# Half of the mixer's output projection taken into the attention stage, as plain fp32 products with the residual beside them

## The chip, the cores and the metric

One core of one Trainium2 chip runs the whole program. The metric is device time in microseconds (us). Engine names are those of the profile: PE is TensorE, DVE is VectorE, ACT is ScalarE, POOL is GpSimd, SP is the engine that issues most transfers.

## The reference, cut to what matters

The program is a long chain of stages: two mixing blocks over 1024 tokens of 1024 features, then a block with two feed-forward layers and, between them, a mixer with sparse attention. The change concerns the mixer and the residual behind it:

```python
def _mixer(h, w_in, kv_norm_g, w_uk, w_uv, gln_g, gln_b, ws, bs, w_out, topk):
    proj = h @ w_in
    q, c, qi, ki, wi, z = jnp.split(proj, SPLITS, axis=-1)
    ...
    att = _sparse_attention(q, c, qi, ki, wi, w_uk, w_uv, topk)   # 512 features, 8 heads
    gm = _chunked_gmlp(z, gln_g, gln_b, ws, bs)                   # 512 features, "gated"
    return jnp.concatenate([att, gm], axis=-1) @ w_out            # 1024 x 1024

# in second_block, with DEEPNORM_ALPHA = 2 ** 0.25
m = _mixer(x, ...)
x = _layernorm(DEEPNORM_ALPHA * x + m, ln2_g[l], ln2_b[l])
```

So `m = att @ w_out[0:512] + gm @ w_out[512:1024]`. The gated half `gm` depends on nothing that attention computes.

## The kernel before, in words

Activations lie with features on the 128 partitions: `xT` is 128 x 8 x 1024 (eight groups of 128 features, all tokens), and `mT`, the mixer's output, has the same shape. Groups 0 to 3 of `mT` hold the queries and are overwritten, block of 128 tokens by block, with attention's result. Groups 4 to 7 hold the gated half, which is complete when the stage before attention ("in_2") ends.

A dense product is done in three terms. Weights and activations are split into a high part (a copy in the format fp32r, on ACT) and a low part (the remainder, on DVE), and `product` (L280 to L282) issues high x high, high x low and low x high for each group of 128 input features.

**Attention** (`mixer_stage`, block "attention") walks over 8 blocks of 128 queries with 8 heads each, two heads per step: 32 steps and two to drain. Per step s, PE computes the scores of two heads as plain fp32 products over 64 rows (`score`, L3378), turns the probabilities of two heads (`turn`, L3390) and multiplies them with the values (`value`, L3400). DVE adds the mask and finds the minimum (`add`, L3577); ACT does the exponential with its sum (`exponent`, L3486) and copies the turned probabilities out of PSUM (`turned`, L3475). After each block of four steps the inverse sums are turned and spread (L3410, L3417, L3492, L3499) and the block is rescaled (L3589). In the first 16 steps (blocks 0 to 3, "NARROW") each row of scores fits one PSUM bank, four banks rotate, and scores are computed one step ahead of that. From step 16 on a row takes two banks and two rows rotate.

Beside that runs a bitwise search for the top 256 keys of each query of the later blocks. A round is asked on DVE (`rank_ask`, L2966), partly answered on ACT (`sign_round`, L2984), and finished on DVE (L2974, L2976). Which round belongs to which head is fixed beforehand (`ROUNDS_AT`): within steps 0 to 15 there are 20 rounds, and in ten of these steps one lies between ACT's two exponentials.

Each engine works through its own list in the written order and waits at semaphores. Nothing is reordered at run time between the engines' lists.

**The projection** (`combine_stage`, called as "out_2") multiplies `mT` with `w_out`: 16 items, eight output groups for tokens 0 to 511 and then eight for tokens 512 to 1023, each with 8 input groups x 3 terms = 24 products of 512 columns. Per item ACT and DVE cut the weights of the item two further on (L245, L248), DVE adds the result to the residual (`deepnorm_update`, L707: `x = x * ALPHA + product`) and adds up the layer norm's mean (L201, L204). During the second eight items DVE also centres the first 512 tokens (L491), adds their squares (L454, L459), inverts (L497) and scales (L505), as `early_dve` orders. The next stage starts when this has ended.

Of the kernel before, what the change touches and what calls it, by code (L numbers as in the profile page):

```python
# [8 lines left out]
P = 128  # L9
D = 1024  # L10
KD = D // P
# [71 lines left out]
def program(nc, A):  # L83
# [18 lines left out]
    with root:  # L102
# [195 lines left out]

        def load_following(ring, sp, n_tiles, following):
            for m in range(2 if following else 0):  # L300
                ring.load(sp, n_tiles // 2, m, following[m])

# [304 lines left out]

        def combine_stage(name, ring, w_dram, rhs, chunks, groups, update, squares, norm, primed, following, cut=Cut):

            items = [(gi, m) for gi in range(len(groups)) for m in range(KD)]  # L610
            n_items = len(items)
            with ExitStack() as ctx:
                parts = Parts(ctx, name, KD, chunks[-1][0] + chunks[-1][1])
                totals = Totals(ctx, name, chunks, squares, groups)
                norm.totals = totals
                head = cut(rhs, parts, KD, chunks)
                with nc.Block(name) as block:
                    @block.sync
                    def _(sp):
                        for i, (gi, m) in enumerate(items):  # L620
                            if i >= 2 or not primed:
                                ring.load(sp, i // 2, i % 2, w_dram[m])
                            if i == 1:
                                head.on_sp(sp)
                        load_following(ring, sp, n_items, following)

                    @block.scalar
                    def _(act):
                        def finish(i):
                            gi, m = items[i]  # L630
                            if squares:
                                act.wait_ge(evacuated[i % 2].h, evacuated[i % 2].base + i // 2 + 1)
                                totals.square(act, gi, m)
                        steps = in_turn(n_items, lambda i: ring.cut_high(act, i // 2, i % 2), finish, primed, following)
                        head.lead_act(act)
                        next(steps)
                        head.on_act(act, [0])
                        for i, _ in enumerate(steps):
                            if i == 1:
                                head.on_act(act, range(1, len(chunks)))  # L640
                            norm.early_act(act, i, totalled.base)

                    @block.vector
                    def _(dve):
                        def finish(i):
# [11 lines left out]
                        steps = in_turn(n_items, lambda i: ring.cut_low(dve, i // 2, i % 2), finish, primed, following)  # L657
                        head.lead_dve(dve)
# [8 lines left out]
                    def _(pe):  # L667
# [6 lines left out]
                        for i, (gi, m) in enumerate(items):  # L674
# [3 lines left out]
                            for c in groups[gi]:  # L678
# [2227 lines left out]
        def mixer_stage(mT, ring, head, following):  # L2906
# [29 lines left out]
            with ExitStack() as mixer:  # L2936
# [381 lines left out]
                rs = sb(mixer, "at_rs", [P, 2, NH])  # L3318
                rT = sb(mixer, "at_rT", [NH, P])
                N = NQ * NH  # L3320
                PAIRS = N // 2
# [4 lines left out]
                def row_at(n):  # L3326
                    return n % 4 * 512 if n < NARROW else n % 2 * SEQ

                def rows_behind(n):
# [26 lines left out]
                with nc.Block("attention") as block:  # L3356
                    @block.sync
                    def _(sp):
                        sp.dma_start(causal[:, P:2 * P], A["later"]).then_inc(S["a_loaded"], 16)
                        sp.dma_start(xT[0:NH, 4:6, SEQ:T], A["heads_out"].rearrange("h (k j) t -> h k (j t)", k=2))\  # L3360
                            .then_inc(S["a_loaded"], 16)
                        sp.wait_ge(S["a_keys"], NH // 2)
                        load_following(ring, sp, 0, following)

                    @block.tensor
                    def _(pe):
                        def score(p):
                            b, j = p // 4, p % 4
                            if 2 * p < NARROW:
                                if p >= 2:  # L3370
                                    pe.wait_ge(S["a_added"], 2 * (p - 1))
                            else:
                                pe.wait_ge(S["a_added"], 2 * p)
                            for c in range(0, (b + 1) * P, 512):
                                w = min(512, (b + 1) * P - c)
                                for i in range(2):
                                    at, hp = row_at(2 * p + i) + c, slice(64 * i, 64 * i + 64)
                                    last = nc.tensor.matmul(PS[:, at:at + w], mT[hp, j, b * P:b * P + P],  # L3378
# [34 lines left out]
                        def spread_inverse(b):  # L3413
# [4 lines left out]
                            last.then_inc(S["a_transposed"], 1)  # L3418

                        pe.wait_ge(S["a_weights"], 32)  # L3420
                        for k in range(NQ):
# [37 lines left out]
                    def _(act):  # L3459
# [34 lines left out]
                        def inverse_spread(b):  # L3494
                            t = place["spread", b, 0]
                            act.wait_ge(S["a_transposed"], t + 1)
                            if b:
                                act.wait_ge(S["a_rescaled"], b)
                            nc.scalar.activation(spread, bank(4 + t % 2).rearrange("p (k t) -> p k t", k=2), ACT.Copy)\  # L3499
                                .then_inc(S["a_turned"], 1)  # L3500

                        for s in range(STEPS + 1):
                            if 0 <= s - 1 < PAIRS:
                                turned(2 * s - 2)
                                turned(2 * s - 1)
# [10 lines left out]
                            if s - PRIMED_FROM in (0, 1):  # L3516
                                ring.cut_high(act, 0, s - PRIMED_FROM)

                    @block.vector
                    def _(dve):  # L3520
# [48 lines left out]
                        def add(n):  # L3569
# [5 lines left out]
                            if rows_behind(n) >= 0:  # L3575
                                dve.wait_ge(S["a_exp"], rows_behind(n) + 1)
                            nc.vector.tensor_tensor_reduce(  # L3577
                                out=sm[:, at:at + w], in0=PS[:, at:at + w], in1=bias, scale=1.0, scalar=3.0e38,
                                op0=ALU.add, op1=ALU.min, accum_out=mn[:, n % 4:n % 4 + 1]).then_inc(S["a_added"], 1)
# [16 lines left out]
                        for s in range(STEPS + 1):  # L3596
# [21 lines left out]
                            if s - PRIMED_FROM in (0, 1):  # L3618
                                ring.cut_low(dve, 0, s - PRIMED_FROM)
                        link.end()  # L3620


# [106 lines left out]
        with ExitStack() as seam:  # L3729
# [114 lines left out]
```

## Time and profile before

| | |
|---|---|
| three runs | 3782.5, 3794.1 and 3795.0 us, median 3794.1 us |
| profiled execution | span 3783.3 us from the first to the last instruction; the page gives no other time of it |
| attention's steps 0 to 15 | about 2749.8 to 2828.6 us of the span |
| attention's end | about 2964 us |
| the projection, first product to last sum | 2965.6 to 3059 us |
| TensorE's mean granted clock | 0.953 of full |

The start of a stretch is read from the timeline (the first instruction of a line), its work from the windows (busy time per engine and the granted clock in that stretch), and an engine's reason for standing still from the list of waits. Matmuls are pipelined: a row's own duration includes the time for the result to drain, so the rate of a run of matmuls is read from the distance between starts.

### The profile page before, as it was taken

The page shows a single profiled execution, that of the slowest core. Times are in us where ns is not written, and L with a number is a line of the kernel's source. Part 1 is how long each engine was busy: PE and PEld are TensorE (multiplying, and loading weights), DVE is VectorE, ACT ScalarE, POOL GpSimd, SP SyncE. Part 2 cuts the span into 40 slices and gives each one's busy share as a digit, 9 for nine tenths or more (in the row PEclk, how much of TensorE's full clock was granted, in tenths as well). Part 3 has the DMA queues.
Part 4 walks back from the last instruction along what each step waited for, and adds up shares of the span by engine and source line. Part 5 has one row for each costly group of instructions (what it writes and reads, how often), then busy time and mean ns, then how long its engine had stood idle before and what let it go on. Part 6 is the DMA issues. An engine that isn't in the chain of part 4 may idle for free. (4 is left out here: it accounts for less than half of the span.)

```text
span 3783.3 us, 67165 instructions
## 1 busy us (share of the span) xinstructions
PE 3357.8 (89%) x28642; PEld 2684.9 (71%) x28642; DVE 2569.7 (68%) x3589; ACT 1265.4 (33%) x2021; POOL 269.8 (7%) x235
## 2 busy tenths in 40 slices
PE   2999898999757877869999999989977999999997
PEld 1888686887426777737888888767735777888885
DVE  7566447572456676645977777767786588777777
ACT  2211222223434333323422222235465443222223
POOL 0000000000000000000111111020000001111110
PEclk9999999999869899979999999999968999999998
DMA  4233311132382233132111111111000121111111
GB/s 186 98 111 114 133 62 45 67 108 82 134 282 55 58 82 82 49 141 86 54 51 57 61 51 51 39 46 34 18 12 1 62 72 51 52 51 51 51 51 56
DMA packets 151062, 278.38 MB, mean 74 GB/s; under 512 B 9836, under 2 KB 82684, under 8 KB 150508
## 3 DMA queue, kind: packets, MB, share of 16 engines
q1 hardware_dynamic: 135468, 244.50, 19.5%
q10 hardware_dynamic: 15296, 29.57, 2.2%
q8 instruction: 228, 3.74, 0.4%
q14 instruction: 70, 0.57, 0.1%
HBM read 228.11 MB, written 45.65 MB: 72 GB/s over the span
## 5 line engine op out<-in xcount | busy, mean ns | idle before, releaser
L2518 PE MATMUL PS<-ffn_x_low_again,ring_b_wh 128*128 128x512 f32 x1120 | 436.0, 389 | 0.0
L2517 PE MATMUL PS<-ffn_x_high,ring_b_wh 128*128 128x512 f32 x1120 | 436.0, 389 | 0.0
L2767 DVE SCALAR_TENSOR_TENSOR xT<-xT,PS 128x1024 f32<-128x1024 f32 (+1 forms) x320 | 368.2, 1162 | 5.3 <-PE PS L2527 0.2
L248 DVE TENSOR_TENSOR ring_a_wl<-ring_a_raw,ring_a_wh 128x1024 fp32r<-128x1024 f32 x72 | 88.2, 1225 | 340.2 <-ACT ring_a_wh L245 339.9
L2750 DVE TENSOR_TENSOR xT<-xT,PS 128x512 f32<-128x512 f32 x280 | 188.1, 683 | 120.6 <-PE PS L2519 119.1
L245 ACT ACTIVATE ring_a_wh<-ring_a_raw 128x1024 fp32r<-128x1024 f32 x72 | 76.1, 1058 | 571.5 <-PE PS L282 547.2
L2525 PE MATMUL PS<-ffn_hid_high,ffn_down_high 128*128 128x512 f32 x640 | 253.2, 396 | 3.7 <-DVE xT L2767 3.2
L245 ACT ACTIVATE ring_b_wh<-ring_b_raw 128x512 fp32r<-128x512 f32 (+1 forms) x156 | 120.4, 773 | 388.7 <-PE PS L2519 252.9
L2526 PE MATMUL PS<-ffn_hid_low,ffn_down_high 128*128 128x512 f32 x640 | 250.3, 391 | 0.0
L2527 PE MATMUL PS<-ffn_hid_high,ffn_down_raw_again 128*128 128x512 f32 x640 | 250.2, 391 | 0.0
L2517 PEld LDWEIGHTS PS<-ffn_x_high,ring_b_wh 128*128 128x128 f32 x1120 | 210.3, 188 | 43.7
L2518 PEld LDWEIGHTS PS<-ffn_x_low_again,ring_b_wh 128*128 128x128 f32 x1120 | 210.3, 188 | 43.7
L280 PE MATMUL PS<-in_o_high,ring_a_wh 128*128 128x512 f32 (+1 forms) x608 | 230.5, 379 | 11.5 <-DVE in_o_low L543 6.3
L281 PE MATMUL PS<-in_o_low,ring_a_wh 128*128 128x512 f32 (+1 forms) x608 | 227.9, 375 | 0.0
L282 PE MATMUL PS<-in_o_high,ring_a_wl 128*128 128x512 f32 (+1 forms) x608 | 227.8, 375 | 0.0
L280 PE MATMUL PS<-in_e_high,ring_a_wh 128*128 128x512 f32 (+1 forms) x576 | 208.6, 362 | 14.4 <-DVE in_e_low L543 13.0
L281 PE MATMUL PS<-in_e_low,ring_a_wh 128*128 128x512 f32 (+1 forms) x576 | 204.8, 356 | 0.0
L282 PE MATMUL PS<-in_e_high,ring_a_wl 128*128 128x512 f32 (+1 forms) x576 | 204.7, 355 | 0.0
L2519 PE MATMUL PS<-ffn_x_high,ring_b_raw_again 128*128 128x512 f32 x416 | 161.9, 389 | 0.0
L2519 PE MATMUL PS<-ffn_x_high,ring_b_wl 128*128 128x512 f32 x392 | 152.6, 389 | 0.0
L248 DVE TENSOR_TENSOR ring_b_wl<-ring_b_raw,ring_b_wh 128x1024 fp32r<-128x1024 f32 x52 | 63.6, 1225 | 126.0 <-ACT ring_b_wh L245 126.0
L245 ACT ACTIVATE ring_b_wh<-ring_b_wl_again 128x512 fp32r<-128x512 f32 x98 | 61.9, 632 | 257.6 <-PE PS L2519 257.6
(507 smaller groups left out, 7767.3 us busy)
## 6 DMA issues: line engine op xcount, KB each, us to landing
ffn_down_raw<-in_ffn_down SPq DMA_DIRECT2D x40, 512.0 KB, 3.5
scan_tin<-scan_in SPq DMA_DIRECT2D x36, 512.0 KB, 5.3
norm_e_t<-in_ada SPq DMA_DIRECT2D x32, 512.0 KB, 4.0
ring_a_raw<-in_in_o SPq DMA_DIRECT2D x32, 512.0 KB, 4.4
ring_b_raw<-in_ffn_up SPq DMA_DIRECT2D x58, 256.0 KB, 4.5
ring_b_wl_again<-in_ffn_up SPq DMA_DIRECT2D x56, 256.0 KB, 4.3
scan_in<-um SPq DMA_DIRECT2D x20, 641.0 KB, 9.4
ring_a_raw<-in_in_e SPq DMA_DIRECT2D x24, 512.0 KB, 3.5
```

The lines of the kernel that those rows point to most:

```text
L245: return nc.scalar.activation(out, x, ACT.Copy)
L280: nc.tensor.matmul(out, wh, xh, start=k == 0, stop=False)
L281: nc.tensor.matmul(out, wh, xl, start=False, stop=False)
L282: last = nc.tensor.matmul(out, wl, xh, start=False, stop=k == kt - 1)
L2517: nc.tensor.matmul(out, wh[:, k, :], xh[:, o, k], start=k == 0, stop=False)
L2518: nc.tensor.matmul(out, wh[:, k, :], xl[:, o, k], start=False, stop=False)
L2519: last = nc.tensor.matmul(out, wl[:, k, :], xh[:, o, k], start=False, stop=k == KH - 1)
L2525: nc.tensor.matmul(out, wh[:, m, :], a, start=n == 0, stop=False)
L2526: nc.tensor.matmul(out, wh[:, m, :], b, start=False, stop=False)
L2527: last = nc.tensor.matmul(out, wl[:, m, :], a, start=False, stop=n == len(us) - 1)
L2750: nc.vector.tensor_tensor(out, x, two(up_bank(q, i)), ALU.add).then_inc(combined.h, 1)
L2767: nc.vector.scalar_tensor_tensor(x, x, ALPHA if q == N_PLAIN else 1.0, out, ALU.mult, ALU.add)\
```

## The change

The gated half of the projection leaves "out_2" and is done in attention's steps 0 to 15. One transfer brings the matching half of `w_out` (2 MB). For each of the 16 pieces (output group x half of the tokens) PE issues four plain fp32 products of 512 columns over full 128 rows and a fifth with `grown`, the identity matrix times ALPHA, over `xT`. ACT copies each finished piece back to `xT` (`keep_part`). The pieces use PSUM banks 2 and 3; the score rows of steps 0 to 15 keep banks 0 and 1 only (`bank_at`), so scores are computed one step less ahead. "out_2" keeps four input groups (`kt=KD // 2`), and its update adds without ALPHA.

```diff
-        def combine_stage(name, ring, ..., following, cut=Cut):
+        def combine_stage(name, ring, ..., following, cut=Cut, kt=KD):
...
-                                last = ring.product(pe, PS[:, at:at + w], s, parts, 0, KD, t, w, ready if m == 0 else None)
+                                last = ring.product(pe, PS[:, at:at + w], s, parts, 0, kt, t, w, ready if m == 0 else None)
...
+                        sp.dma_start(gated_w[:, :, :, :], A["w_out"][:, :, KD // 2:KD].rearrange("m p k t -> p m k t"))\
+                            .then_inc(gated_in.h, 16)
...
                         def score(p):
                             b, j = p // 4, p % 4
-                            if 2 * p < NARROW:
-                                if p >= 2:
-                                    pe.wait_ge(S["a_added"], 2 * (p - 1))
-                            else:
+                            if p:
                                 pe.wait_ge(S["a_added"], 2 * p)
...
+                        def gated_part(n):
+                            i, k = divmod(n, KD // 2 + 1)
+                            c, m = divmod(i, KD)
+                            t, w = MAIN_CHUNKS[c]
+                            out = bank(2 + i % 2)
+                            if k == 0:
+                                if i == 0:
+                                    pe.wait_ge(gated_in.h, gated_in.base + 16)
+                                    pe.wait_ge(grown_made.h, grown_made.base + 1)
+                                if i >= 2:
+                                    pe.wait_ge(part_kept.h, part_kept.base + i - 1)
+                            if k < KD // 2:
+                                nc.tensor.matmul(out, gated_w[:, m, k, :], mT[:, KD // 2 + k, t:t + w], start=k == 0, stop=False)
+                            else:
+                                nc.tensor.matmul(out, grown[:, :], xT[:, m, t:t + w], start=False, stop=True)\
+                                    .then_inc(part_done.h, 1)
...
                         score(0)
-                        score(1)
+                        gated_parts(5)
                         pe.wait_ge(S["a_loaded"], 32)
                         for s in range(STEPS):
-                            if NARROW // 2 <= s + 1 < PAIRS:
+                            if s + 1 < PAIRS:
...
                                 score(s + 1)
+                            gated_parts(1)
                             if s < PAIRS:
                                 turn(2 * s)
                                 turn(2 * s + 1)
-                            if s + 2 < NARROW // 2:
-                                score(s + 2)
+                            gated_parts(2)
                             if 0 <= s - 1 < PAIRS:
                                 value(s - 1)
+                            gated_parts(2)
...
+                        def keep_part(i):
+                            c, m = divmod(i, KD)
+                            t, w = MAIN_CHUNKS[c]
+                            act.wait_ge(part_done.h, part_done.base + i + 1)
+                            nc.scalar.activation(xT[:, m, t:t + w], bank(2 + i % 2), ACT.Copy).then_inc(part_kept.h, 1)
+
+                        nc.scalar.activation(grown[:, :], ident[:, :], ACT.Copy, scale=ALPHA).then_inc(grown_made.h, 1)
                         for s in range(STEPS + 1):
+                            if s < NARROW // 2:
+                                keep_part(s)
                             if 0 <= s - 1 < PAIRS:
                                 turned(2 * s - 2)
                                 turned(2 * s - 1)
...
-                combine_stage("out_2", ring, A["w_out"], mT, MAIN_CHUNKS, BY_CHUNK, deepnorm_update, False, ln2, True, A["ffn2_up"])
+                combine_stage("out_2", ring, A["w_out"], mT, MAIN_CHUNKS, BY_CHUNK,
+                              lambda m, t, w, at: deepnorm_update(m, t, w, at, 1.0), False, ln2, True, A["ffn2_up"], kt=KD // 2)
```

PE's list before, at block 2 of attention (`at_keys` are scores, `at_pr` turns, `at_values` values, `at_rs` and `at_rT` the inverse sums):

```order
L3390 MATMUL PS<-ident,at_pr 128x128 x6
L3378 MATMUL PS<-at_keys,mT 128x384 x2
L3400 MATMUL PS<-at_pT,at_values 64x128 x4
L3410 MATMUL PS<-ident,at_rs 8x128
L3390 MATMUL PS<-ident,at_pr 128x128 x6
L3378 MATMUL PS<-at_keys,mT 128x384 x2
L3400 MATMUL PS<-at_pT,at_values 64x128 x6
```

PE's list now at the same place (`at_gated_w` are the four products of a piece, `at_grown` the identity product):

```order
L3385 MATMUL PS<-at_keys,mT 128x384 x2
L3439 MATMUL PS<-mT,at_gated_w 128x512
L3397 MATMUL PS<-ident,at_pr 128x128 x6
L3439 MATMUL PS<-mT,at_gated_w 128x512 x2
L3407 MATMUL PS<-at_pT,at_values 64x128 x4
L3439 MATMUL PS<-mT,at_gated_w 128x512
L3441 MATMUL PS<-xT,at_grown 128x512
L3417 MATMUL PS<-ident,at_rs 8x128
L3385 MATMUL PS<-at_keys,mT 128x384 x2
L3439 MATMUL PS<-mT,at_gated_w 128x512
L3397 MATMUL PS<-ident,at_pr 128x128 x6
L3439 MATMUL PS<-mT,at_gated_w 128x512 x2
```

Each step's score has moved from behind the turns to the front of the step, where it is waited for at once, and five products stand in three gaps: one ahead of the turns, two ahead of the values and two behind them.

ACT's list before, at the end of block 1 and the beginning of block 2 (`at_pT` the turned probabilities, `at_pr` the exponentials, `rank_signs` a round's answer):

```order
L3475 ACTIVATE at_pT<-PS 128x2x128 x2
L3486 ACTIVATE at_pr,at_rs<-at_rows,at_mn 128x384
L2984 ACTIVATE rank_signs,rank_found<-at_score,rank_cand 128x1024
L3486 ACTIVATE at_pr,at_rs<-at_rows,at_mn 128x384
L3475 ACTIVATE at_pT<-PS 128x3x128 x2
L3492 ACTIVATE at_rT<-PS 8x128
L3486 ACTIVATE at_pr,at_rs<-at_rows,at_mn 128x384
L2984 ACTIVATE rank_signs,rank_found<-at_score,rank_cand 128x1024
```

ACT's list now at the same place (a write of `xT` with 128x512 is `keep_part`):

```order
L3541 ACTIVATE xT<-PS 128x512
L3510 ACTIVATE at_pT<-PS 128x2x128 x2
L3521 ACTIVATE at_pr,at_rs<-at_rows,at_mn 128x384
L2986 ACTIVATE rank_signs,rank_found<-at_score,rank_cand 128x1024
L3521 ACTIVATE at_pr,at_rs<-at_rows,at_mn 128x384
L3541 ACTIVATE xT<-PS 128x512
L3510 ACTIVATE at_pT<-PS 128x3x128 x2
L3527 ACTIVATE at_rT<-PS 8x128
L3521 ACTIVATE at_pr,at_rs<-at_rows,at_mn 128x384
```

A copy that waits for PE's fifth product of a piece now heads every step, ahead of the two copies of turned probabilities and of both exponentials.

## Rows read from the trace of the kernel before

**Rows 1.** The page's first lines: the span, then busy time of each engine.
```profile
span 3783.3 us, 67165 instructions
...
PE 3357.8 (89%) x28642; PEld 2684.9 (71%) x28642; DVE 2569.7 (68%) x3589; ACT 1265.4 (33%) x2021; POOL 269.8 (7%) x235
```

**Rows 2.** Windows over attention: length, busy time per engine, granted clock, DMA.
```profile
2750.00:2830.00 80.00, 58.62 (x295) 32.82 (x295) 68.05 (x190) 54.07 (x140) 0.00 (x0) 0.64 0.04 13
...
2758.00:2776.00 18.00, 15.01 (x65) 7.86 (x65) 15.90 (x51) 11.66 (x37) 0.00 (x0) 0.50 0.00 1
...
2875.00:2965.00 90.00, 71.22 (x648) 50.19 (x648) 41.54 (x74) 53.16 (x107) 0.00 (x0) 0.95 0.00 1
```

**Rows 3.** Waits of PE in 2750 to 2830: total us, times, longest.
```profile
PE PS L3390 <- ACT at_pr L3486: 21.4, 19, 3.0
```

**Rows 4.** Windows over the projection.
```profile
2980.00:3020.00 40.00, 40.00 (x174) 32.45 (x174) 23.30 (x30) 11.81 (x16) 0.00 (x0) 1.00 0.27 92
3020.00:3058.00 38.00, 37.88 (x166) 30.68 (x164) 30.62 (x37) 12.27 (x13) 0.00 (x0) 1.00 0.25 83
```

**Rows 5.** Timeline of PE, plain fp32: start, us, engine, line, operation.
```profile
2741.53 7.03 PE L3430 MATMUL PS<-at_cT,ring_b_raw 128*128 128x512 f32 x16
...
2804.11 1.13 PE L3378 MATMUL PS<-at_keys,mT 64*128 64x512 f32 x4
```

**Rows 6.** Timeline of PE in the projection, split terms.
```profile
2965.63 0.76 PE L280 MATMUL PS<-out_high,ring_b_wh 128*128 128x512 f32 x1 [3.23 <-DVE out_low L248]
...
2990.01 0.39 PE L281 MATMUL PS<-out_low,ring_b_wh 128*128 128x512 f32 x1
2990.24 0.39 PE L282 MATMUL PS<-out_high,ring_b_wl 128*128 128x512 f32 x1
...
3058.66 1.13 PE L212 MATMUL PS<-out_totals,avg 128*128 128x512 f32 x2 [0.78 <-DVE xT L707]
```

**Rows 7.** Timeline of ACT in attention's steps 0 to 15.
```profile
2760.21 0.42 ACT L3475 ACTIVATE at_pT<-PS 128x128 f32<-128x128 f32 x2
2761.67 0.40 ACT L3486 ACTIVATE at_pr<-at_rows,at_mn 128x128 f32<-128x128 f32 x1 [1.03 <-DVE at_mn L3577]
...
2822.48 0.60 ACT L3499 ACTIVATE xT<-PS 128x512 f32<-128x512 f32 x1 [3.24 <-PE PS L3417]
...
2824.81 0.71 ACT L3486 ACTIVATE at_pr<-at_rows,at_mn 128x512 f32<-128x512 f32 x1
2825.42 0.19 ACT L3486 ACTIVATION_READ_ACCUMULATOR at_pr<-at_rows,at_mn 128x1 f32 x1
...
2828.07 1.14 ACT L2984 ACTIVATE rank_signs<-at_score,rank_cand 128x1024 int8<-128x1024 f32 x1
...
2831.57 1.09 ACT L3475 ACTIVATE at_pT<-PS 128x512 f32<-128x512 f32 x2 [0.44 <-PE PS L3390]
```

**Rows 8.** Timeline of DVE around and in the projection.
```profile
2964.79 4.91 DVE L248 TENSOR_TENSOR out_low<-mT,out_high 128x512 fp32r<-128x512 f32 x8 [0.96 <-ACT out_high L245]
...
2996.58 1.23 DVE L248 TENSOR_TENSOR ring_b_wl<-ring_b_raw,ring_b_wh 128x1024 fp32r<-128x1024 f32 x1 [2.89 <-ACT ring_b_wh L245]
2997.72 0.68 DVE L707 SCALAR_TENSOR_TENSOR xT<-xT,PS 128x512 f32<-128x512 f32 x1
...
3020.54 4.61 DVE L491 TENSOR_TENSOR xT<-xT,PS 128x1024 f32<-128x1024 f32 x4
...
3028.81 4.47 DVE L459 TENSOR_TENSOR out_totals<-out_totals,xT 128x512 f32<-128x512 f32 x6
...
3045.22 3.34 DVE L497 RECIPROCAL norm_std<-norm_std 128x512 f32<-128x512 f32 x1
...
3050.87 2.73 DVE L505 SCALAR_TENSOR_TENSOR xT<-xT,vec,norm_std 128x512 f32<-128x512 f32 x4
```

**Rows 9.** SP's issue ahead of the new transfer; DMA issues in 2700 to 3000.
```profile
2734.92 0.78 SPq L3360 DMA_DIRECT2D xT<-in_heads_out  x1
...
ring_b_raw<-in_w_out SPq DMA_DIRECT2D x9, 512.0 KB, 3.3
```

More of the change, by code:

```diff
@@ L297, in in_turn, with load_following @@
                 yield
-        def load_following(ring, sp, n_tiles, following):
+        def load_following(ring, sp, n_tiles, following, kt=KD):
             for m in range(2 if following else 0):
-                ring.load(sp, n_tiles // 2, m, following[m])
+                ring.load(sp, n_tiles // 2, m, following[m][:, 0:kt], kt)
         cen_ready, sq_ready, std_ready = sem("cen_ready"), sem("sq_ready"), sem("std_ready")
@@ L606, in end, with combine_stage @@
                     pool_step.base += n * KD
-        def combine_stage(name, ring, w_dram, rhs, chunks, groups, update, squares, norm, primed, following, cut=Cut):
+        def combine_stage(name, ring, w_dram, rhs, chunks, groups, update, squares, norm, primed, following, cut=Cut, kt=KD):
             items = [(gi, m) for gi in range(len(groups)) for m in range(KD)]
@@ L612, in combine_stage @@
             with ExitStack() as ctx:
-                parts = Parts(ctx, name, KD, chunks[-1][0] + chunks[-1][1])
+                parts = Parts(ctx, name, kt, chunks[-1][0] + chunks[-1][1])
                 totals = Totals(ctx, name, chunks, squares, groups)
                 norm.totals = totals
-                head = cut(rhs, parts, KD, chunks)
+                head = cut(rhs, parts, kt, chunks)
                 with nc.Block(name) as block:
@@ L621, in _ @@
                             if i >= 2 or not primed:
-                                ring.load(sp, i // 2, i % 2, w_dram[m])
+                                ring.load(sp, i // 2, i % 2, w_dram[m][:, 0:kt], kt)
                             if i == 1:
@@ L633, in finish @@
                                 totals.square(act, gi, m)
-                        steps = in_turn(n_items, lambda i: ring.cut_high(act, i // 2, i % 2), finish, primed, following)
+                        width = lambda i: kt if i < n_items else KD
+                        steps = in_turn(n_items, lambda i: ring.cut_high(act, i // 2, i % 2, width(i)), finish, primed, following)
                         head.lead_act(act)
@@ L656, in finish @@
                                 totals.add(dve, gi, m)
-                        steps = in_turn(n_items, lambda i: ring.cut_low(dve, i // 2, i % 2), finish, primed, following)
+                        width = lambda i: kt if i < n_items else KD
+                        steps = in_turn(n_items, lambda i: ring.cut_low(dve, i // 2, i % 2, width(i)), finish, primed, following)
                         head.lead_dve(dve)
@@ L3418, in spread_inverse, with gated_parts @@
                             last.then_inc(S["a_transposed"], 1)
+                        def gated_part(n):
[14 more added lines that the diff above has]
+                                    .then_inc(part_done.h, 1)
+                        PART_STEPS = 2 * KD * (KD // 2 + 1)
+                        part_steps = iter(range(PART_STEPS))
+                        def gated_parts(n):
+                            for at in itertools.islice(part_steps, n):
+                                gated_part(at)
                         pe.wait_ge(S["a_weights"], 32)
@@ L3516, in _ @@
                             if s - PRIMED_FROM in (0, 1):
-                                ring.cut_high(act, 0, s - PRIMED_FROM)
+                                ring.cut_high(act, 0, s - PRIMED_FROM, KD // 2)
                     @block.vector
@@ L3577, in add @@
                             nc.vector.tensor_tensor_reduce(
[L3578 removed]
+                                out=sm[:, at:at + w], in0=PS[:, bank_at(n):bank_at(n) + w], in1=bias, scale=1.0, scalar=3.0e38,
                                 op0=ALU.add, op1=ALU.min, accum_out=mn[:, n % 4:n % 4 + 1]).then_inc(S["a_added"], 1)
@@ L3618, in _ @@
                             if s - PRIMED_FROM in (0, 1):
-                                ring.cut_low(dve, 0, s - PRIMED_FROM)
+                                ring.cut_low(dve, 0, s - PRIMED_FROM, KD // 2)
                         link.end()
+                gated_in.base += 16
+                grown_made.base += 1
+                part_done.base += 2 * KD
+                part_kept.base += 2 * KD
         def mod_cols(w):
```

12 lines of the change are left out of this document (10 added, 2 removed).

## The prediction

> **What bounds the kernel now.** I read the page first. PE is busy for 89% of the span [rows 1], so work taken from PE should count. But that is a mean over stages, and the change takes work from one stage and puts it into another, so both have to be read apart.
>
> The windows show two different stages. In the projection PE is busy in every microsecond at full clock, and DVE is busy for 23.3 of 40 us in its first part but for 30.6 of 38 in its second [rows 4]. So PE bounds it, with DVE not far behind in the second half. In attention's steps 0 to 15 (80 us) DVE is busy for 68 us, PE for 58.6 and ACT for 54, with PE's granted clock at 0.64 of full [rows 2]. DVE with its rounds sets the pace, and PE's longest wait is for ACT's exponentials, 21.4 us in 19 waits [rows 3]. PE looks like a place with room. How much room is the question: 58.6 us at 0.64 of the clock are 58.6 x 0.64 = 37.5 us of work at the full level, so at most 80 - 37.5 = 42.5 us are free, and only if the clock rises.
>
> **What the new work costs on PE.** A plain fp32 product of 512 columns over 128 rows is two entries of the trace: the eight such products of the keys, 16 entries, take 7.03 us, the last one's drain included [rows 5]. I take 0.855 us each. A term of the split product starts every 0.227 us (2990.01 to 2990.24) [rows 6], so three take 0.68 us. Plain fp32 is therefore dearer on PE than the three terms it replaces, by 0.17 us per group. 16 pieces x 4 products x 0.855 = 54.7 us, and the 16 identity products, which replace nothing on PE, add 13.7: 68.4 us go into attention. 16 x 4 x 3 = 192 terms x 0.227 = 43.6 us leave the projection.
>
> **Attention, steps 0 to 15.** PE's work becomes 37.5 + 68.4 = 106 us in a stage that lasts 80. So PE is the bound of this stage, and DVE's rounds, 68 us of work, are covered. That alone is +26 us. (The 37.5 holds some drain that overlaps the next start, a few us; I leave it in.)
>
> On top come waits, because the order gives PE and ACT a loop in every step. ACT's step begins with the copy of the piece whose fifth product ends PE's step before. Behind that copy on ACT wait two copies of turned probabilities, the first exponential, in ten of 16 steps a round's answer, and the second exponential; PE's turns wait for the exponentials. In the meantime PE has only the next score and one product. In block 3: ACT needs 0.6 for the piece's copy (a copy of 512 columns out of PSUM), 1.09 for two copies, 0.71 + 0.19 for the exponential with its sum [rows 7]; less about 0.3 where ACT overlaps the ends of neighbouring entries and plus about 0.3 of drain and signals, 2.6 us. PE covers a score of 1.13 [rows 5], some 1.05 of it before the next start, and 0.855: 1.9. The wait is 0.7. The second turn comes 0.7 later by its exponential, of which the first turn covers some 0.5, and 1.14 later still in ten of 16 steps [rows 7], 0.7 on average: 1.6 us per step. In block 0 the copies are 0.42 and the exponential 0.40 [rows 7], so 1.65 us stand against a small score (an estimate of 0.3, a quarter of block 3's columns) and 0.855: 0.5, then 0.2 and 0.7, so 1.4. A mean of 1.5 x 16 = 24 us. The inverse sums' turn and spread now also wait behind that copy, in six steps, but that wait mostly comes out of the next one, and I add nothing.
>
> The sum is 106 + 24 = 130 us against 80: **+50 us**. From below, with the waits gone, it is +26; from above it depends on the clock (the rival below). Nothing gives it back later: steps 16 on keep their order, and the rounds are fixed to heads, so a slower step does not advance any.
>
> Smaller edits. Losing the score that ran ahead costs nothing more, since DVE, no longer the bound, has added both rows long before PE comes to the score; without that cover it would be a score and a signal per step, 1 us x 16. The identity matrix is one ACT copy beside table loading, under 0.6 us. The 2 MB transfer is issued behind one at 2734.92 and is needed at about 2750; at the 512 KB in 3.3 us of the ring's loads [rows 9] four times that is 13.2 us, just in time; it could cost 0 to 3 us and I take 0. Halved cuts of the first two weights near attention's end save 1 us at most.
>
> **The projection.** It runs from 2965.6 to the last sum at 3058.7, 93 us [rows 6]. Per item PE falls from 24 x 0.227 = 5.45 to 2.73 us. On DVE the cut of the weights halves, from 1.23 [rows 8] to that of a 512-column row, 4.91 / 8 = 0.61, and update and sum stay at 0.68 each (less overlap, 0.6; the sum has the update's shape): 1.8 us per item. In the first eight items that is under 2.73, so PE stays the bound: 21.8 us, and 1 for the four rows of the second chunk that DVE cuts in between, and 2.6 for the slow first twelve terms (the row at 2965.63 shows 0.76 instead of 0.39). In the second eight items DVE has the norm as well: eight updates 4.9, seven sums 4.0, six cuts 3.7 and two full ones for the next stage 2.3, centring 4.6, seven additions of squares 5.1, reciprocal 3.3, four of the eight scalings 2.7 [rows 8]: 30.6 us against PE's 21.8. **DVE becomes the bound there**, and with its waits for ACT's squares and root, 3 to 5 us by estimate, the half takes about 35. So 21.8 + 1 + 2.6 + 35 = 60.4, against 93: **-32 us**, not -43.6. Bounds: -43.6 if DVE keeps up, -26 if its waits double.
>
> **Sum.** +50 - 32 = **+18 us**. The span of 3783.3 becomes 3801; the median of the runs shown, 3794.1, lies 10.8 above that span, so I forecast 3812. From below +26 - 32 = -6, from above see the clock.
>
> **Clock.** In attention's first part the granted clock is 0.64, and 0.50 in 2758 to 2776, the lower level throughout, though PE was busy for 15 of 18 us; in its last part, with 71 of 90 us busy and pauses of under a microsecond, it is 0.95 [rows 2]. Now PE works some 106 of 130 us, like that last part, so I take the full level. The Trainium skill, "TensorE: Matmul & The Clock Gate", section "A second HAM failure mode: psum-queue depth-cycling", says that short pauses between groups of products can make the clock swing between both levels and that throughput suffers from it. By that rule the new stage, with its one or two pauses per step, would swing too; the 0.64 agrees with it and the 0.95 speaks against it for a stage as full as this one.
>
> **Rivals.**
> - *PE is the only bound in both stages* (faster). If ACT's chain fits under the score and the one product, attention costs +26, and if DVE keeps up, the projection gives -43.6: -18, 3776 us. It decides once the chain is under 1.2 us in block 0 and 1.9 in block 3. Rows 3 speak for room on ACT's side; the chain of 1.65 and 2.6 us and the 30.6 us on DVE speak against. With the chain covered but DVE as worked out it is -6, 3788.
> - *The clock falls*. If PE runs a fifth slower on average, its 106 us become 127: +71 - 32 = +39, 3833 us. If it stays at the lower level, 212 + 24 - 80 = +156, far outside. The rows at 0.50 speak for it, the 0.95 against.
> - *The change does not do what it says*: the transfer lands late and PE stands behind the first score; 3 us more, inside the range.
>
> **How the numbers follow.** My forecast (+5 to +32, 3799 to 3826) has 0.60; the clock's loss 0.13; the chain covered but DVE the bound 0.17; PE alone the bound 0.10. The range 3785 to 3838 leaves out the far end of the clock's case and most of the faster one. 0.3% is 11 us, about what a measurement can tell from no change (the three runs span 12). Slower by more: 0.13 and four fifths of 0.60, 0.61. Same: the rest of that 0.60, 0.12, and 0.17, so 0.29. Faster: 0.10.
>
> **What would show it.** Steps 0 to 15 should last about 130 us with PE's waits at the turns, behind ACT, and the granted clock near 1. The plain products should start every 0.43 us per entry. ACT should stand still for PE's identity product. In the projection terms should keep their 0.227 us in items 0 to 7, and PE should wait for DVE in items 8 to 15. I am wrong if steps 0 to 15 last under 110 us, or the projection under 52.

## The result, and the profile after

The changed kernel takes 3808.4 us (median of four runs, 3803.5 to 3810.0) against 3794.6 for before (four runs, 3782.5 to 3795.6). The ratio is 1.0043, 95% interval 1.0029 to 1.0056: slower by 16 us (11 to 21). The forecast was 3812.

The page of the changed kernel, first lines:

```profile
span 3808.2 us, 67105 instructions
...
PE 3367.1 (88%) x28610; PEld 2660.1 (70%) x28610; DVE 2557.4 (67%) x3581; ACT 1261.8 (33%) x2030; POOL 273.2 (7%) x235
```

PE is busy for 9 us more than in [rows 1], in a span that is 25 us longer. 4 us of the 25 lie ahead of attention, in code that is the same in both kernels: the start of attention differs by up to 15 us among the profiles of this study. So I compare three stretches that the timeline marks by their first instructions: from the first score to score 16 (steps 0 to 15), from there to the projection's first product, and from there to the last sum (L212). The windows of the changed kernel over these three stretches, and those of before (length, busy time of PE, weight loads, DVE, ACT and POOL, granted clock, DMA share, GB/s):

```profile
2753.91:2882.30 128.39, 111.54 (x452) 49.06 (x452) 68.41 (x187) 58.51 (x149) 0.00 (x0) 1.00 0.01 4
2882.30:3021.36 139.06, 100.72 (x837) 70.10 (x838) 80.14 (x156) 79.86 (x167) 0.00 (x0) 0.88 0.01 2
3021.36:3082.78 61.42, 52.63 (x199) 40.15 (x199) 48.31 (x69) 19.50 (x28) 0.00 (x0) 0.91 0.23 75
```

```profile
2749.77:2828.61 78.84, 57.46 (x291) 32.20 (x291) 67.58 (x187) 52.91 (x136) 0.00 (x0) 0.64 0.04 14
2828.61:2965.63 137.02, 100.21 (x840) 69.76 (x838) 81.22 (x156) 78.91 (x163) 0.00 (x0) 0.87 0.01 2
2965.63:3058.66 93.03, 92.25 (x391) 74.79 (x391) 60.85 (x76) 29.41 (x36) 0.00 (x0) 0.97 0.26 90
```

So attention's first part lasts 49.6 us longer, its second 2.0, and the projection is 31.6 shorter: +20.0 in all. In steps 0 to 15 DVE's busy time has hardly changed, ACT's has grown by 5.6 us, PE's has nearly doubled, and the granted clock has gone from 0.64 to 1.00.

PE's timeline at attention's start (start, duration, engine, line, operation, in brackets the idle time ahead and who ended it):

```profile
2753.91 0.49 PE L3385 MATMUL PS<-at_keys,mT 64*128 64x128 f32 x4 [1.21 <-ACT at_keys L3500]
2754.33 3.70 PE L3439 MATMUL PS<-mT,at_gated_w 128*128 128x512 f32 x8
2757.87 1.02 PE L3441 MATMUL PS<-xT,at_grown 128*128 128x512 f32 x2
...
2768.44 0.33 PE L3397 MATMUL PS<-ident,at_pr 128*128 128x128 f32 x1 [1.18 <-ACT at_pr L3521]
...
2778.81 0.70 PE L3385 MATMUL PS<-at_keys,mT 64*128 64x256 f32 x4
2779.45 1.12 PE L3439 MATMUL PS<-mT,at_gated_w 128*128 128x512 f32 x2
2780.41 0.58 PE L3397 MATMUL PS<-ident,at_pr 128*128 128x128 f32 x2
2780.83 1.88 PE L3439 MATMUL PS<-mT,at_gated_w 128*128 128x512 f32 x4
2782.64 0.44 PE L3407 MATMUL PS<-at_pT,at_values 128*64 128x128 f32 x4
2783.01 1.12 PE L3439 MATMUL PS<-mT,at_gated_w 128*128 128x512 f32 x2
2783.97 1.02 PE L3441 MATMUL PS<-xT,at_grown 128*128 128x512 f32 x2
2784.93 0.70 PE L3385 MATMUL PS<-at_keys,mT 64*128 64x256 f32 x4
```

The first piece starts right behind the first score, so the 2 MB had landed. Its eight entries take 2757.87 - 2754.33 = 3.54 us; from the second on they start 0.43 us apart, as the forecast said. In the loop the five products of a piece take more. In the step from 2778.81, where PE waits for nothing, they hold PE for 0.96 (from 2779.45), 1.81 (from 2780.83) and 1.92 us (from 2783.01), each counted to the start of what follows: 4.69 us, 0.94 per product. That is some 0.1 us more at each of the four changes to or from a score or a value. The row at 2768.44 is a wait of the kind that the forecast worked out: the second turn stands still for its exponential. The waits of steps 0 to 15 (who waits for whom: us in total, times, longest):

```profile
ACT xT L3541 <- PE PS L3441: 67.0, 16, 5.4
...
PE PS L3397 <- ACT at_pr L3521: 8.0, 9, 1.2
...
PE PS L3417 <- ACT at_pT L3510: 3.5, 3, 1.3
PE PS L3424 <- ACT at_pT L3510: 3.2, 3, 1.2
...
PE PS L3385 <- DVE at_mn L3621: 1.3, 1, 1.3
```

ACT stands for 67 of 128 us at the head of its step, waiting for the identity product, and PE then waits for ACT: 8.0 us for exponentials at nine of the turns, and 6.7 us for turned copies at the six turns and spreads of the inverse sums. ACT's timeline shows what queues behind that copy:

```profile
2792.59 0.60 ACT L3541 ACTIVATE xT<-PS 128x512 f32<-128x512 f32 x1 [3.28 <-PE PS L3441]
2793.08 0.66 ACT L3510 ACTIVATE at_pT<-PS 128x256 f32<-128x256 f32 x2
2793.91 0.27 ACT L3527 ACTIVATE at_rT<-PS 8x128 f32<-8x128 f32 x1 [0.17 <-PE PS L3417]
2794.09 0.49 ACT L3521 ACTIVATE at_pr<-at_rows,at_mn 128x256 f32<-128x256 f32 x1
```

In the projection, the windows of its two halves (the ninth item's first product starts at 3046.64) and, for the experiments, of what lies behind its first 28.64 us; then PE's waits in all of it, and DVE's in the second half:

```profile
3021.36:3046.63 25.27, 24.18 (x96) 19.54 (x97) 17.26 (x28) 7.20 (x13) 0.00 (x0) 0.91 0.23 79
3046.63:3082.78 36.15, 28.45 (x104) 20.61 (x102) 31.05 (x42) 12.30 (x15) 0.00 (x0) 0.91 0.23 73
```

```profile
3050.00:3082.78 32.78, 25.08 (x90) 17.97 (x88) 29.54 (x39) 11.29 (x14) 0.00 (x0) 0.90 0.21 66
```

```profile
PE PS L280 <- DVE xT L709: 4.2, 3, 2.0
PE PS L280 <- DVE out_low L248: 3.2, 1, 3.2
PE PS L465 <- DVE out_totals L459: 2.8, 1, 2.8
PE PS L212 <- DVE xT L709: 1.8, 1, 1.8
```

```profile
DVE ring_b_wl L248 <- ACT ring_b_wh L245: 4.4, 3, 2.3
```

In the second half DVE works for 31.1 of 36.2 us, and PE's waits there, 7.7 us, are all for DVE. (The 3.2 us lie ahead of the first product, and one wait of 1.1 us lies in the first half.) In [rows 4] PE had next to no pause.

### The profile page after: what moved, and what is told of

Its sections match the earlier page's. It is cut to its first block and busy times, and to the rows that moved or that the text cites. A ratio compares the mean times of both kernels' runs of the same rounds, so it can differ in the third digit from the quotient of the medians.

```text
span 3808.2 us, 67105 instructions
## 1 busy us (share of the span) xinstructions
PE 3367.1 (88%) x28610; PEld 2660.1 (70%) x28610; DVE 2557.4 (67%) x3581; ACT 1261.8 (33%) x2030; POOL 273.2 (7%) x235
## 5 line engine op out<-in xcount | busy, mean ns | idle before, releaser
L2519 PEld LDWEIGHTS PS<-ffn_x_high,ring_b_wh 128*128 128x128 f32 x1120 | 210.2, 188 | 43.6
L2527 PEld LDWEIGHTS PS<-ffn_hid_high,ffn_down_high 128*128 128x128 f32 x640 | 121.1, 189 | 32.3 <-issue 5.7
```

The source lines that it names most:

```text
L2519: nc.tensor.matmul(out, wh[:, k, :], xh[:, o, k], start=k == 0, stop=False)
L2527: nc.tensor.matmul(out, wh[:, m, :], a, start=n == 0, stop=False)
```

## The experiments

All were timed against before on the same chip. "Stage" is the sum of the three stretches in the profiled run. Two profiles of the changed kernel give 328.9 and 329.2 us; a single stretch of unchanged code can differ by 3 us (steps 0 to 15 of c2_more_dve). Whole runs of before differ by up to 16 us.

| kernel | steps 0-15 | to the projection | projection | stage | against before | ratio to before (95%) |
|---|---|---|---|---|---|---|
| before | 78.8 | 137.0 | 93.0 | 308.9 | | |
| changed | 128.4 | 139.1 | 61.4 | 328.9 | +20.0 | 1.0043 (1.0029-1.0056) |
| a1_gated_only | 128.4 | 140.2 | 92.3 | 360.9 | +52.0 | 1.0143 (1.0129-1.0158) |
| a2_projection_only | 78.9 | 136.1 | 62.2 | 277.1 | -31.8 | 0.9905 (0.9893-0.9918) |
| a3_keep_late (the changed kernel) | 128.4 | 139.2 | 61.6 | 329.2 | +20.3 | 1.0054 (1.0042-1.0066) |
| a4_dve_residual | 101.8 | 135.2 | 61.6 | 298.5 | -10.4 | 0.9967 (0.9955-0.9979) |
| b1_keep_tail | 110.9 | 136.6 | 61.3 | 308.8 | 0.0 | 0.9990 (0.9980-0.9999) |
| b2_order_only | 80.4 | 135.0 | 93.2 | 308.7 | -0.2 | 0.9995 (0.9987-1.0004) |
| b3_more_pe | 128.4 | 139.1 | 61.8 | 329.3 | +20.4 | 1.0055 (1.0043-1.0067) |
| b4_first_chunk | 87.8 | 134.0 | 78.7 | 300.5 | -8.4 | 0.9975 (0.9967-0.9984) |
| c1_second_chunk | 87.8 | 135.0 | 82.2 | 305.0 | -3.9 | 0.9982 (0.9973-0.9991) |
| c2_more_dve | 131.5 | 139.0 | 66.1 | 336.6 | +27.7 | 1.0056 (1.0044-1.0069) |

**The two halves of the change.** One kernel has the new attention and the old projection:

```diff
-  lambda ...: deepnorm_update(m, t, w, at, 1.0), False, ln2, True, A["ffn2_up"], kt=KD // 2)
+  lambda ...: deepnorm_update(m, t, w, at, 1.0), False, ln2, True, A["ffn2_up"])
```

> The changed kernel, but with the projection of before (all eight groups), so the gated half is counted twice; the first part of attention alone carries the cost. Theory (the two places of the change are independent: attention +50, projection -32): before +50, about 3844 (3839 to 3849). Rival 1 (the projection is worth what its fp32r products lasted, 43.6, and attention therefore costs 60): before +58 to +60, about 3853. Rival 2 (attention costs only the products that TensorE gets more, 106 - 80 = 26, and the rest of the difference between the traces is their spread): before +26 to +30, about 3822.

The other is before with the short projection:

```diff
-  combine_stage("out_2", ..., deepnorm_update, False, ln2, True, A["ffn2_up"])
+  combine_stage("out_2", ..., deepnorm_update, False, ln2, True, A["ffn2_up"], kt=KD // 2)
```

> Attention as before, the projection with the four groups of attention's heads alone; the gated half of the sum is left out altogether. Theory (VectorE sets the pace of the projection's second half): before -32, about 3763 (3758 to 3768). Rival 1 (TensorE is all that counts there): before -44, about 3751. Rival 2 (the projection gains more in this place than the two traces show, because the clock falls in the changed one): -36 to -40.

Measured: +52.0 us in the stage and +54 (49 to 60) by the ratio for attention alone; -31.8 and -36 (-41 to -31) for the projection alone. The two add to the change's own +20.0 within 0.3. The ratio intervals also reach the rivals at +58 and at -36 to -40; the stretches decide against them: attention costs 49.6 + 3.2, and the projection without the new attention lasts 62.2 us, no shorter than the 61.4 of the changed kernel. A saving of 44 is refuted by a2_projection_only, by both measures.

**ScalarE's copy.** The run a3_keep_late was meant to move the copy, but its file held the changed kernel without the edit. Its expectation is void, and it serves as a second measurement of the changed kernel:

> The changed kernel with ScalarE's copy of a finished piece at the end of its step instead of the head; nothing else differs. Theory (the copy heads ScalarE's step and waits there for the identity product, on which TensorE has just been working, so the turns and exponentials behind it come late and TensorE waits 17 us for them in steps 0 to 15): those waits go, -12 to -20 against the changed kernel, about 3793. Rival (TensorE's own work, 111.5 of the 128.1 us of steps 0 to 15, and the score held back until VectorE has read the last one set the step; ScalarE's wait is slack): 0 to -4 against the changed kernel, 3804 to 3808.

The edit itself ran as b1_keep_tail:

```diff
                         for s in range(STEPS + 1):
-                            if s < NARROW // 2:
-                                keep_part(s)
                             if 0 <= s - 1 < PAIRS:
...
+                            if s < NARROW // 2:
+                                keep_part(s)
                             if s - PRIMED_FROM in (0, 1):
```

> The changed kernel with ScalarE's copy of a finished piece moved from the head to the end of its step (the run a3_keep_late held the changed kernel itself, the edit was missing there). Theory (at the head the copy waits for TensorE's whole step, 15 waits of 4 us by the trace, and the turned copies and exponentials behind it start late, so TensorE waits 17 us for them in steps 0 to 15): steps 0 to 15 last 104 to 114 us instead of 128.4, -14 to -24 against the changed kernel, about 3790, no longer slower than before. Rival (TensorE's own work, 111.5 us, and other waits set the step): 0 to -4, steps 0 to 15 at 125 to 128.

Measured: steps 0 to 15 last 110.9 us, 17.5 less, and the whole gain against the changed kernel is 20 us of stage. Its window over steps 0 to 15 and its waits there:

```profile
2743.85:2854.74 110.89, 107.98 (x451) 49.70 (x452) 70.65 (x193) 63.72 (x158) 0.00 (x0) 1.00 0.02 5
```

```profile
ACT xT L3541 <- PE PS L3441: 9.8, 8, 2.8
...
PE PS L3397 <- ACT at_pr L3521: 2.2, 4, 0.7
```

PE is now busy for 108 of 110.9 us. ACT's 67 us at the copy have become 9.8, PE's 8.0 at the turns 2.2, and the waits at L3417 and L3424 are gone. That the place of ACT's copy costs 17.5 us is shown; the rival, that PE's own work sets all of the 128, falls. Of PE's 108 us the 80 products of the pieces hold 74.3, each entry of the timeline counted to the start of the next, and everything else 33.6. What is left, 110.9 - 78.8 = 32 us, is PE's work, and the projection's 31.7 pay for just that.

**The scores that no longer run ahead.** The new order and banks, without any piece:

```diff
-                        gated_parts(5)
...
-                            gated_parts(1)
...
-                            gated_parts(2)
```

> Attention in the changed kernel's order and with its two score banks, but without any piece (no gated products, identity products, copies or 2 MB transfer); the projection as before. Only the lost run-ahead of the scores is left of the change. Theory (priced at nothing in the forecast; VectorE reads a score soon after it is made): before 0 to +4, steps 0 to 15 at 79 to 83 us. Rival (each score now waits for VectorE, 1 us in 16 steps): before +16, steps 0 to 15 at 95.

Measured: steps 0 to 15 last 80.4 us, 1.6 more, which the next stretch gives back; by the ratio -2 (-5 to +2). The zero in the forecast stands, though not for its reason. Without the pieces PE has no cover, and the forecast would then have charged 1 us x 16. But PE's wait only moves, from the exponentials (21.4 us in [rows 3]) to the scores, and DVE is as busy as before. The window over steps 0 to 15, and PE's wait there:

```profile
2746.45:2826.89 80.44, 56.77 (x291) 33.68 (x291) 67.74 (x188) 54.92 (x138) 0.00 (x0) 0.64 0.04 13
```

```profile
PE PS L3383 <- DVE at_mn L3611: 22.1, 12, 4.0
```

The granted clock is 0.64 here, as in before, and 1.00 in the changed kernel. So it is the pieces, not the order, that raised it.

**Which engine holds the projection's second half.** Two kernels add about the same time to one engine each:

```diff
+                                if kt < KD and gi == 1:
+                                    ...
+                                    for _ in range(3):
+                                        nc.tensor.matmul(PS[:, at:at + w], ring.high[:, s, 0, :], parts.high[:, 0, t:t + w],
+                                                         start=True, stop=True)
                                 last = ring.product(pe, PS[:, at:at + w], s, parts, 0, kt, t, w, ...)
```

> The changed kernel with three more fp32r products (0.68 us) ahead of each of the eight items of the projection's second half, 5.4 us of TensorE's time in all, overwritten by the item's own first product. Theory (VectorE sets the pace there, 30.6 us of work against 21.8 on TensorE): the time from the projection's first product to its last sum stays at 61.4 to 62.5 us, 0 to +1 against the changed kernel. Rival (TensorE and VectorE take turns, and TensorE's share of each turn counts): +5, 66 to 67 us.

```diff
+                                if kt < KD and gi == 1:
+                                    nc.vector.scalar_tensor_tensor(idle[:, 0:w], xT[:, m, t:t + w], 1.0,
+                                                                   PS[:, s * 1536 + t:s * 1536 + t + w], ALU.mult, ALU.add)
                                 last = update(m, t, w, s * 1536 + t)
```

> The changed kernel with one more VectorE instruction in each of the eight items of the projection's second half, of the residual's form (0.68 us, 5.5 us in all) into a tile that nobody reads. The counterpart of b3_more_pe, where 5.4 us more on TensorE moved the projection from 61.4 to 61.8 us. Theory (VectorE sets the pace of the second half): projection 66 to 67 us, +5 against the changed kernel, about 3813 to 3816. Rival (neither engine does, but the hand-over between them): 61.8 to 64 us.

What lies behind the projection's first 28.64 us, with more on PE and then with more on DVE:

```profile
3047.25:3080.38 33.13, 27.58 (x112) 20.37 (x112) 29.54 (x39) 11.67 (x14) 0.00 (x0) 1.00 0.20 66
```

```profile
3054.47:3091.89 37.42, 27.29 (x89) 19.37 (x88) 34.25 (x47) 11.43 (x14) 0.00 (x0) 0.86 0.18 58
```

24 more products cost 0.35 us, eight more DVE instructions 4.64 of their 4.7 us. DVE sets the pace there. The whole-run ratio of c2 does not show the 4.6 us beside the noise of the runs; its profiled run also had a clock of 0.96 in steps 0 to 15, ahead of the edit, where PE was busy for 116 us instead of 111.5 and the stretch lasted 131.5.

**The residual on VectorE.** No identity product and no copy on ACT; DVE adds as the projection does:

```diff
-                            if k < KD // 2:
-                                nc.tensor.matmul(out, gated_w[:, m, k, :], ..., start=k == 0, stop=False)
-                            else:
-                                nc.tensor.matmul(out, grown[:, :], xT[:, m, t:t + w], start=False, stop=True)\
-                                    .then_inc(part_done.h, 1)
+                            last = nc.tensor.matmul(out, gated_w[:, m, k, :], ..., start=k == 0, stop=k == KD // 2 - 1)
...
+                            dve.wait_ge(part_done.h, part_done.base + i + 1)
+                            deepnorm_update(m, t, w, (2 + i % 2) * 512).then_inc(part_kept.h, 1)
```

> The changed kernel without the 16 identity products and without ScalarE's copies: VectorE adds the piece to the scaled residual (one instruction of about 0.68 us per piece) at the end of its step; TensorE has four products a piece. Theory: TensorE loses 16.3 us of identity products, and ScalarE's step no longer waits for a piece, which takes most of the 17 us of waits as well: -25 to -30 against the changed kernel, about 3781, so before -13. Rival 1 (only the products go, the waits stay): -16, about 3792. Rival 2 (VectorE, with 11 us more and a wait for each piece in its own step, holds the next scores back): -5 to +5 against the changed kernel.

Measured: the stage is 30.4 us shorter than the changed kernel's and 10.4 shorter than before's; by the ratio -13 us (-17 to -8) against before, as its expectation had it. This kernel beats both. Its steps 0 to 15:

```profile
2753.29:2855.05 101.76, 95.53 (x419) 44.11 (x420) 80.11 (x209) 55.12 (x141) 0.00 (x0) 0.98 0.02 6
```

PE is busy for 12.5 us less than in b1_keep_tail and the stretch is 9.1 shorter; by its 95.5 of 101.8 us PE still bounds it, and DVE, busy for 80.1 us instead of 68.4, fits beside it.

**Half of the pieces.** The same with one half of the tokens only, two products a step:

```diff
-                        PART_STEPS = 2 * KD * (KD // 2)
+                        PART_STEPS = KD * (KD // 2)
...
-  lambda ...: deepnorm_update(m, t, w, at, 1.0), ..., kt=KD // 2)
+  lambda ...: deepnorm_update(m, t, w, at, 1.0 if t < 512 else ALPHA), ..., kts=(KD // 2, KD))
```

> As a4_dve_residual, but only the eight pieces of the first 512 columns are done in attention, two products a step; the projection takes four groups in its first half and eight in the second. Theory (before's attention leaves TensorE some 20 us free in steps 0 to 15 and runs it there at a lower clock, so the first 33 us of products cost little, +4 to +10; the second half of the projection was held by VectorE when it had four groups and loses little by having eight, the first half saves 17 to 22): before -10 to -16, about 3781, level with a4_dve_residual. Rival 1 (attention's products cost their full time, +23 to +33): before +3 to +12. Rival 2 (attention takes them for nothing): before -20.

> As b4_first_chunk, but the eight pieces are those of the second 512 columns: the projection takes eight groups in its first half and four in its second. Theory (the stages' times add: in a4 and b4 the second half's four groups were worth 78.7 - 61.6 = 17.1 us, the first half's 93.0 - 78.7 = 14.3; eight pieces cost attention 5.9 in b4): projection about 76, before -11 in the stage from the first score to the last sum, about 3778 in all. Rival (the second half is VectorE's, so four groups there give at most (43.6 / 2) - 30.6 + 21.8 = 13 us less, and the first half's VectorE work, freed in b4, was the rest): projection at 80 or more, before -7 or less.

Windows of b4_first_chunk over steps 0 to 15 and over the first half of its projection, a wait of PE in that half, and the window over the second half of c1's projection:

```profile
2751.51:2839.31 87.80, 70.81 (x356) 35.42 (x356) 72.31 (x195) 53.88 (x136) 0.00 (x0) 0.92 0.02 6
2973.29:3004.78 31.49, 27.60 (x97) 21.79 (x97) 19.80 (x32) 9.90 (x18) 0.00 (x0) 0.80 0.23 81
```

```profile
PE PS L280 <- DVE xT L709: 3.5, 1, 3.5
```

```profile
3023.81:3060.11 36.30, 28.60 (x104) 20.72 (x102) 30.83 (x41) 12.30 (x15) 0.00 (x0) 0.91 0.20 66
```

The first eight pieces cost steps 0 to 15 only 9.0 us (87.8 - 78.8), and 5.9 with the stretch behind; the second eight cost 14.0 more (101.8 - 87.8). The expectation for b4 held for attention (+4 to +10) but not for the projection, which saved 14.3 us instead of 17 to 22: by the stage -8.4, short of -10 to -16, by the ratio -9 (-13 to -6). The one for c1 did not hold: its projection lasts 82.2 us, not 76.

The traces show why the two savings, 14.3 and 10.8, fall short of 31.6. In before the halves of the projection last 45.9 and 47.1 us. The second half with four groups takes 36.2 us in the changed kernel and 36.3 in c1: it saves 11 us in both, with DVE busy for about 31, and the rival, that DVE holds this half, had it right. (The forecast's terms for c1, 43.6 + 1 + 2.6 and 35, meet its 82.2 by chance, since its halves last 45.9 and 36.3.) The first half with four groups takes 25.3 us in the changed kernel, which saves 20.6, but 31.5 in b4. There DVE cuts eight rows of the second chunk between two updates instead of four (4.90 us instead of 2.49), and PE waits 3.5 us for it instead of 1.1. During this wait the clock fell to its lower level for 6.8 us, in which 13 terms started 0.43 us apart instead of 0.227, an estimated 2.6 us. These two are about 5 of the 6.2 us. Both kernels are a little faster than before, and neither beats a4_dve_residual by the stage.

## Why the prediction was right

Its mechanisms are the ones that the runs show, but the size of its largest term is in part luck: two misses of opposite sign nearly cancel.

- **Attention, +50.** Measured +49.6 for steps 0 to 15. The forecast had 106 us of work and 24 of waits; the trace has PE busy for 111.5 of the 128.4 us and idle for 16.9.
  - *The work.* A product was priced well (0.43 us per entry), but not the 0.1 us at each change to or from a score or a value: 80 products hold PE for 74.3 us in b1, not 68.4. Against that, everything else holds it for 33.6, not 37.5; the drain that the forecast knowingly left in is probably part of that difference. So b1 shows 108. The 3.5 us more in the changed kernel are probably ends of products ahead of PE's waits, which nothing overlaps.
  - *The waits.* All 24 us were to lie at the turns, 0.5 to 0.7 us at the first turn of every step and 0.9 at the second. The turns have 8.0, in nine waits, and in one step alone the first turn is among them; 6.7 lie at the inverse sums' turn and spread, which the forecast put at nothing. So ACT's chain did mostly fit under the score and one product, as the rival asked; what did not fit was the second exponential and the inverse sums. That ACT's copy at the head of the step is behind these waits was the forecast's mechanism, and b1 shows it, with 17.5 us.
  - *The stretch behind.* "Nothing gives it back later" was too simple: the stretch behind lasted 2.0 us longer in the changed kernel and 0.4 to 2 less in kernels without ACT's early copy (b1, a4, b2); with 136.1 in a2, whose attention is that of before, about 1 us of it is spread.
- **The zeros.** The lost run-ahead of the scores cost nothing (b2), and in the changed kernel PE waits once for a score's rows to be read, 1.3 us. The transfer cost nothing (first gated product at 2754.33, right behind the first score).
- **The projection, -32.** Measured -31.6 (61.4 us against the forecast's 60.4), and -30.8 alone in a2. Its terms hold one by one: the first half lasts 25.3 us (forecast 25.4), the second 36.2 (35), with 31.1 us of DVE's work in it (30.6). DVE's own waits there, put at 3 to 5 us for ACT's squares and root, are 4.4, but for ACT's cuts of the weights. That DVE bounds its second half is shown by b3 and c2.
- **The clock.** It was granted at 1.00 in steps 0 to 15, as assumed, and b2 shows that the pieces raised it. The likeness that the forecast took it from was misread: in the last part of before's attention, at 0.95 [rows 2], PE's pauses are not all under a microsecond. Two waits for DVE alone make 7.7 us:

```profile
PE PS L3378 <- DVE at_mn L3577: 7.7, 2, 4.4
```

  The Trainium skill's rule on swings between the two levels ("TensorE: Matmul & The Clock Gate", "A second HAM failure mode: psum-queue depth-cycling") was weighed as the rival; with PE pausing for up to 1.3 us in most steps no such swing shows in this stage of the changed kernel, only a 0.96 in one of the profiled runs (c2). In the projection's second half, where PE waits for up to 2.8 us, the mean is 0.91.
- **The rival "PE is the only bound"** asked for ACT's chain to fit under a score and one product and for DVE to keep up. The copy's place costs 17.5 us, and DVE did not keep up. With the copy moved (b1) the change comes to 0, not to the -6 of the forecast's middle case: 108 instead of 106 us of work, 3 us of waits that remain, and 78.8 us to start from instead of 80.
- **The base.** The forecast added the step to the median of the runs, 10.8 us above the profiled span; the runs' own noise (16 us between the runs of before) is as large as the effect, and only the stretches of the traces show the +20 plainly.

## What to carry to other kernels

Work moved into a stage with idle time on an engine is not free: count what the engine does at the clock it will be granted, then follow the hand-overs in each step. An instruction that waits for another engine's last result must not stand at the head of the step whose results that engine needs next: here one copy's place was worth 17.5 of the 50 us. And when the work leaves a stage, price that stage by the engine that is next in line: 43.6 us of products removed were worth 31.6.

## What the runs showed that I had not expected

The first half of the pieces (32 products, some 30 us by b1's 0.93 each) lengthened steps 0 to 15 by 9 us in b4 and again in c1, while the granted clock rose from 0.64 to 0.92; the second half cost 14. The forecast had not asked whether half would do. With more products on PE the clock was also higher behind the projection's first 28.64 us, 1.00 in b3 against 0.90, so that 24 more products added only 2.5 us of busy time (25.1 to 27.6) instead of the 5.4 that their spacing of 0.227 would give. PE's busy time in a stretch that it does not fill is thus no measure of the work in it, unless the clock beside it is read too.
